# Second attention: low parts of four weight blocks formed on GpSimd in place of VectorE

## The chip, the cores and the metric

One core of one Trainium2 chip runs the whole program: TensorE (PE), VectorE (DVE), ScalarE (ACT), GpSimd (POOL) and SyncE (SP), each with its own instruction stream, kept in step by semaphores. The metric is the device time of one execution in microseconds (us); of several runs the median counts.

## What is computed

A first transformer block (window attention, latent attention, a mixture of 16 experts), then a second block: a state-space mixer, a gated feed-forward network with a short convolution, a forgetting attention ("fox"), another such network, and a final norm. The change lies in the forgetting attention:

```python
def fox_mixer(h, w_in, b_f, w_out):
    proj = h @ w_in
    q = proj[..., :D_MODEL].reshape(Bsz, S, FOX_HEADS, FOX_HEAD_DIM) * (FOX_HEAD_DIM ** -0.5)
    k = proj[..., D_MODEL:2 * D_MODEL].reshape(Bsz, S, FOX_HEADS, FOX_HEAD_DIM)
    v = proj[..., 2 * D_MODEL:3 * D_MODEL].reshape(Bsz, S, FOX_HEADS, FOX_HEAD_DIM)
    f_logit = proj[..., 3 * D_MODEL:]
    log_f = jax.nn.log_sigmoid((f_logit + b_f).astype(f32))
    F = lax.cumsum(log_f, axis=1).transpose(0, 2, 1)
    ...
    def attend_block(args):
        qi, q_blk, Fq = args
        s = jnp.einsum('bhqd,bshd->bhqs', q_blk, k).astype(f32)
        s = s + Fq[..., None] - F[:, :, None, :]
        s = jnp.where(causal, s, -jnp.inf)
        p = jax.nn.softmax(s, axis=-1)
        return jnp.einsum('bhqs,bshd->bqhd', p.astype(v.dtype), v)
    ...
    return o @ w_out
```

with 256 positions, width 1024, 16 heads of 64.

## The kernel before

**Matrices in two parts.** The large float32 products are done as three products of rounded parts: a matrix is its high part (rounded to the format fp32r) plus its low part (what the rounding left), and high x high, low x high and high x low are summed in PSUM. For a weight block ScalarE copies the high part (`apart_high`, line 492) and another engine subtracts it to form the low part in the block's own place (`apart_low`, line 500).

**The weight blocks.** They are numbered n in the list `APART`: 0 to 5 belong to the state-space mixer; 6 to 13 to the forgetting attention. Of these 6 and 7 give the queries, 8 and 9 the keys, 10 and 11 the two halves of the values, 12 and 13 the two halves of the output projection. A block is 128 partitions x 4096 float32 (2 MB); both helpers treat it in two halves of 128x2048. All lie in `ring`, a buffer of six slots; a block takes two of them (raw, later low; and high). SyncE loads a block when TensorE has finished with the products of the block that was there before (`released`), so the loads hang on TensorE and not on who forms a low part. `apart_low` waits for `w_high` (ScalarE's half is written) and raises `w_low0` or `w_low1` (by half), which TensorE waits for ahead of the products of that half.

**TensorE's order** in this stage: queries and keys (`features`, eight signals `fox_mm`, which the Vector and Scalar engines wait for to copy the results out of PSUM), then `values(0, 0, ...)` (block 10, first 128 positions), the eight-column product `gate_rows`, `values(1, 0, ...)` (block 11), and then four waits: `fk_copied`, `fv_copied` 2 (ScalarE has copied both value halves), `nf_ready` 8, `gate_copied`. Then `attention(8, 16, ...)` runs eight steps s = 8 to 15 (four heads each: scores, transposes, products with the values). Beside them stand the value products of the last 128 positions (s = 8 to 11) and the output projection of the first 128 positions (`fox_out`, block 12 at s = 13, block 13 at s = 14 and 15).

**VectorE's order**: low parts of 8 and 9; four copies of the keys (line 2734, each behind `fox_mm` 5 to 8), with the low part of 10 between the second and the third; the low part of 11; then the **bias loop**, lines 2741 and 2743: for each of eight pairs of heads it adds the causal mask to the table `nf` of forget sums (128x256 and 128x512 elements, eight times each, all operands in SBUF: `nf` lies in the work buffer `W`, the mask in `kc`) and signals `nf_ready`. In the attention each step does `inverse`, two `probs_copied`, `maxima` of the step after the next, then `between(s)` with low parts of 12 (s = 8, 9) and 13 (s = 12, 13), then `normalized`.

**ScalarE's order**: high parts of 10 and 11, the value copy `values_copied(0)`, high part of 12, gate copy, `values_copied(1)`, then the exponentials; the high part of 13 stands in halves behind the exponentials of s = 11 and s = 12.

**GpSimd** has its last work before this stage in the state-space mixer (lines 2036 and 2044, ending some 300 us earlier).

The order is written out by hand, and each engine takes its instructions in that order.

Of the kernel before, what the change touches and what calls it, by code (L numbers as in the profile page):

```python
# [239 lines left out]
def build(nc, x, cons, cols, rows, relb, wrt, wff, bf16z, w_in, w_qb, w_kvb, w_o, w_gate, w_up, w_down, ada_w,  # L240
# [5 lines left out]
    with ExitStack() as ctx:  # L246
# [5 lines left out]
        def S(name):  # L252
            if name not in sems:
                sems[name] = ctx.enter_context(nc.semaphore(name))
            return sems[name]
# [192 lines left out]
        def low_at(at):  # L448
# [14 lines left out]


        (_, fqT_, fkT_, fv_, nf_, ft_, PT2_, Rf_) = carve(NC * T, NC * T, NC * T, NT * D, FH * 384, 4 * T, 2 * BANK,
                                                          BANK)
        FOX_END = 3 * NC * T + NT * D + FH * 384 + 4 * T + 3 * BANK
# [27 lines left out]
        def apart_low(eng, n, half):  # L495

            name = APART[n]
            a = slice(half * SLOT // 2, (half + 1) * SLOT // 2)
            eng.wait_ge(S("w_high"), 2 * n + half + 1)
            eng.tensor_tensor(ringr[:, slot_of[name], a], ring[:, slot_of[name], a],  # L500
                              ringr[:, high_slot[name], a].bitcast(F32), ALU.subtract
                              ).then_inc(S(f"w_low{half}"), 1)
# [917 lines left out]
        def _(act):  # L1420
# [454 lines left out]
            def fox_high(u):  # L1875

                _, t, half, _ = half_unit(2 * u)
                a, c = slice(t * P, t * P + P), slice(4 * half, 4 * half + 4)
                act.wait_ge(S("o_copied"), 2 * u + 2)
                act.activation(oh[:, c, a], oTf[:, c, a], ACT.Copy).then_inc(S("row_high"), 1)  # L1880
# [23 lines left out]
        def _(pool):  # L1904
# [135 lines left out]
            def kx(ct):  # L2040

                if ct >= 2:
                    pool.wait_ge(S("cy_mm"), ct - 1)
                tt(Kx[:, ct % 2].rearrange("p n (g c) -> p n g c", g=8),
                   Kc[:, ct].unsqueeze(2).to_broadcast([P, SL, 8, S5C]),
                   K("mask8").unsqueeze(1).unsqueeze(3).to_broadcast([P, SL, 8, S5C]), ALU.mult
                   ).then_inc(S("near_ready"), 1)

            for ct in range(NC):
                decay(ct)  # L2050
                kx(ct)


        @block.vector
        def _(v):
# [671 lines left out]
            for half in range(2):  # L2727
                apart_low(v, 9, half)
            for j in range(4):
                if j == 2:  # L2730
                    for half in range(2):
                        apart_low(v, 10, half)
                v.wait_ge(S("fox_mm"), 5 + j)
                v.tensor_copy(fkT[:, 2 * j:2 * j + 2, :], ps[:, 4 + j, :].rearrange("p (c t) -> p c t", c=2)
                              ).then_inc(S("fk_copied"), 1)
            for half in range(2):
                apart_low(v, 11, half)
            v.wait_ge(S("line_spread"), 32)
            for j in range(FH // 2):
                pair = nf[:, 2 * j:2 * j + 2, :]  # L2740
# [6 lines left out]
            def fox_low(u):  # L2747

                _, t, half, _ = half_unit(2 * u)
                a, c = slice(t * P, t * P + P), slice(4 * half, 4 * half + 4)  # L2750
                v.wait_ge(S("row_high"), 2 + u - 3)
                tt(ol[:, c, a], oTf[:, c, a], oh[:, c, a].bitcast(F32), ALU.subtract).then_inc(S("row_low"), 1)

            def fox_between(s):
                if s < 10:
                    apart_low(v, 12, s - 8)
                if s >= 10 and s % 2 == 0:
                    fox_low((s - 2) // 2)
                if s in (12, 13):
                    apart_low(v, 13, s - 12)  # L2760

            attention(8, 16, fox_between)
            fox_low(7)
            for t in range(NT):
# [107 lines left out]
```

## Time and profile before

| | us |
|---|---|
| median of 3 runs | 1361.81 |
| lowest, highest | 1357.71, 1364.49 |
| the profiled execution | 1355.92 |
| its span | 1354.1 |
| TensorE busy in the span | 1202.8 (89%) |
| VectorE busy | 675.1 (50%) |
| ScalarE busy | 449.4 (33%) |
| GpSimd busy | 164.5 (12%) |

The profiled execution lies 5.9 us under the median of the runs. "Busy" is a sum over all stages and tells only who works most; what a change in one stage is worth is read from the stage's own rows: who waits there, for whom, and how long. The stage of the forgetting attention runs from about 1000 us to 1140 us of the span.

### The profile page before, as it was taken

What the parts mean: (1) busy time and instruction counts of PE and PEld (TensorE: products, weight loads), DVE (VectorE), ACT (ScalarE), POOL (GpSimd) and SP (SyncE); (2) the same over time, 40 slices, a digit from 0 to 9 for tenths busy, and PEclk for the clock granted to TensorE, in tenths of its full rate; (3) what the DMA queues carried; (4) which work ended last, traced back from release to release, by engine and by line L of the source; (5) the groups of instructions that cost most, each with busy time, mean ns of one, the idle gap of its engine ahead of it and who ended that gap; (6) DMA issues with size and microseconds to landing.
All of it is one profiled execution on the core that took longest, in us unless ns stands there. A gap on an engine that the chain in (4) does not pass through costs nothing.

```text
span 1354.1 us, 21898 instructions
## 1 busy us (share of the span) xinstructions
PE 1202.8 (89%) x8746; PEld 866.7 (64%) x8746; DVE 675.1 (50%) x1182; ACT 449.4 (33%) x696; POOL 164.5 (12%) x269
## 2 busy tenths in 40 slices
PE   7999889988777988787998979999969987999996
PEld 4645445444233533334866869999959765999995
DVE  2777451212111212214468547666664765677666
ACT  4563412101010100004445244444344444444442
POOL 0000130572343123030110000000000000000000
PEclk9999889878888788778999989999989988999999
DMA  9866899999999999999694235554245222454451
GB/s 363 337 225 265 322 411 427 426 431 427 428 430 427 428 430 427 428 430 389 239 391 182 93 140 186 186 186 186 108 187 205 107 93 94 156 194 184 186 184 43
DMA packets 38100, 371.78 MB, mean 275 GB/s; under 512 B 4102, under 2 KB 7711, under 8 KB 14367
## 3 DMA queue, kind: packets, MB, share of 16 engines
q1 hardware_dynamic: 33552, 364.66, 66.3%
q10 hardware_dynamic: 4494, 6.38, 1.4%
q8 instruction: 38, 0.62, 0.2%
q14 instruction: 16, 0.12, 0.0%
HBM read 369.94 MB, written 1.08 MB: 274 GB/s over the span
## 4 chain that ended last, share of the span: by engine, by line
PE 64%; DMA 25%; DVE 7%; ACT 2%; issue 2%; SPq 0%; DVEq 0%; ACTq 0%
PE ps L666 61%; DMA ring<-in_w_up 21%; DMA ring<-in_ada_w 1%; DMA ring<-in_w_in 1%; PE ps L889 1%; DMA ring<-in_s_out 1%; DMA ring<-in_fox_out 1%; DMA ring<-in_fox_in 1%; PE ps L675 1%; DVE ring_parts L500 1%; DVE W L2743 0%; ACT XH L1487 0%; PE ps L901 0%; DVE XH L2061 0%; DVE W_parts L2658 0%
## 5 line engine op out<-in xcount | busy, mean ns | idle before, releaser
L666 PE MATMUL ps<-W_parts 128*128 128x256 f32 (+2 forms) x2672 | 387.8, 307 | 8.4 <-DVE W_parts L2094 6.1
L666 PEld LDWEIGHTS ps<-W_parts 128*128 128x128 f32 x2672 | 360.6, 193 | 33.5 <-issue 12.0
L666 PE MATMUL ps<-ring,W 128*32 128x512 f32 (+2 forms) x1512 | 238.8, 688 | 55.3 <-DMA ring<-in_w_up 35.0
L666 PEld LDWEIGHTS ps<-ring,W 128*32 128x32 f32 (+1 forms) x1512 | 66.5, 129 | 200.6 <-issue 132.7
L666 PE MATMUL ps<-W 128*32 128x64 f32 (+7 forms) x1696 | 138.6, 298 | 25.3 <-DVE W L2548 14.5
L666 PEld LDWEIGHTS ps<-W 128*32 128x32 f32 (+5 forms) x1696 | 87.6, 157 | 85.4 <-issue 64.4
L2658 DVE TENSOR_TENSOR W_parts<-ring,W_parts 128x2048 fp32r<-128x2048 f32 x44 | 100.9, 2292 | 29.7 <-ACT W_parts L1797 29.7
L666 PE MATMUL ps<-kc,W 128*128 128x32 f32 (+2 forms) x648 | 99.5, 324 | 1.7 <-DVE W L2331 1.0
L666 PEld LDWEIGHTS ps<-kc,W 128*128 128x128 f32 x648 | 99.1, 245 | 2.8 <-DVE W L2331 1.3
L666 PE MATMUL ps<-XH_parts,ring_parts 128*128 128x256 f32 x512 | 94.1, 287 | 5.1 <-issue 5.1
L2537 DVE COPY W<-ps 128x1024 f32<-128x1024 f32 x16 | 19.6, 1224 | 153.8 <-PE ps L666 153.8
L666 PEld LDWEIGHTS ps<-XH_parts,ring_parts 128*128 128x128 f32 x512 | 81.4, 195 | 6.1 <-issue 6.1
L1797 ACT ACTIVATE W_parts<-ring 128x2048 fp32r<-128x2048 f32 x44 | 83.6, 1901 | 0.0
L666 PE MATMUL ps<-ring_parts,W_parts 128*128 128x512 f32 (+1 forms) x256 | 72.7, 403 | 2.2 <-DVE ring_parts L500 2.2
L666 PE MATMUL ps<-W_parts,ring_parts 128*128 128x256 f32 x256 | 73.4, 287 | 0.0
L500 DVE TENSOR_TENSOR ring_parts<-ring,ring_parts 128x2048 fp32r<-128x2048 f32 x28 | 63.1, 2283 | 10.5 <-ACT ring_parts L492 10.5
L492 ACT ACTIVATE ring_parts<-ring 128x2048 fp32r<-128x2048 f32 x28 | 52.1, 1904 | 27.4 <-DMA ring<-in_fox_in 17.3
L1696 ACT ACTIVATE W<-ps 128x1024 f32<-128x1024 f32 x16 | 16.4, 1025 | 133.2 <-PE ps L666 133.2
L2554 DVE TENSOR_TENSOR X<-X,ps 128x512 f32<-128x512 f32 x64 | 44.0, 687 | 28.7 <-PE ps L666 28.7
L666 PEld LDWEIGHTS ps<-ring_parts,W_parts 128*128 128x128 f32 x256 | 49.1, 194 | 13.4 <-DVE ring_parts L500 2.6
L1821 ACT ACTIVATE XH<-ps 128x256 f32<-128x256 f32 x44 | 16.9, 384 | 117.2 <-PE ps L666 117.2
L666 PE MATMUL ps<-ring,silz 128*32 128x512 f32 x384 | 49.8, 641 | 5.2 <-DMA ring<-in_ada_w 5.2
(381 smaller groups left out, 1278.2 us busy)
## 6 DMA issues: line engine op xcount, KB each, us to landing
ring<-in_w_up SPq DMA_DIRECT2D x32, 2048.0 KB, 26.4
ring<-in_w_down SPq DMA_DIRECT2D x32, 2048.0 KB, 21.2
ring<-in_w_gate SPq DMA_DIRECT2D x30, 2048.0 KB, 21.7
ring<-in_ada_w SPq DMA_DIRECT2D x24, 2048.0 KB, 13.1
ring<-in_up SPq DMA_DIRECT2D x44, 1024.0 KB, 5.6
ring<-in_dn SPq DMA_DIRECT2D x44, 512.0 KB, 3.4
ring<-in_fox_in SPq DMA_DIRECT2D x6, 2048.0 KB, 8.6
ring<-in_w_in SPq DMA_DIRECT2D x2, 2048.0 KB, 13.6
```

The lines of the kernel that those rows point to most:

```text
L492: act.activation(ringr[:, high_slot[name], a], ring[:, slot_of[name], a], ACT.Copy).then_inc(S("w_high"), 1)
L500: eng.tensor_tensor(ringr[:, slot_of[name], a], ring[:, slot_of[name], a], ringr[:, high_slot[name], a].bitcast(F32), ALU.subtract).then_i ...
L666: return pe.matmul(o, l, r, start=a, stop=z_, skip_group_check=True, **kw)
L675: last = pe.transpose(ps[:, c // 2, (c % 2) * T + t * P:(c % 2) * T + t * P + P], XN[:, t, c * P:c * P + P], ident)
L889: last = pe.transpose(ps[:, 4 + g % 2, o:o + P], Pex[:, 2 * (g % 4) + h, kb * P:kb * P + P], ident)
L1696: act.activation(Gs.rearrange("p (b n) -> p b n", b=2), ps[:, 0:2, :], ACT.Copy).then_inc(S("g_copied"), 1)
L1797: act.activation(uh[:, b], ring[:, slot_of[name, b], 0:2048].rearrange("p (a n) -> p a n", a=2), ACT.Copy).then_inc(S("up_high"), 1)
L1821: act.activation(apd[:, b, 2:2 + T], ps[:, b, 0:T], ACT.Copy).then_inc(S("a_copied"), 1)
L2537: v.tensor_copy(Us.rearrange("p (b n) -> p b n", b=2), ps[:, 2:4, :]).then_inc(S("u_copied"), 1)
L2554: tt(xs_part, xs_part, ps[:, k, :], ALU.add).then_inc(S("x_added"), 1)
L2658: tt(ul[:, b, :, :], ring[:, slot_of[f"up{k}", b], 0:2 * D].rearrange("p (a n) -> p a n", a=2), uh[:, b, :, :].bitcast(F32), ALU.subtract) ...
```

## The change

The low parts of blocks 10 to 13 (eight instructions of 128x2048) leave VectorE and stand at the end of GpSimd's stream, in the order of the blocks. GpSimd first waits until both halves of all ten earlier low parts are done, so that the counts `w_low0` and `w_low1` keep rising in order.

```diff
@@ GpSimd, at its end
             for ct in range(NC):
                 decay(ct)
                 kx(ct)
+            for half in range(2):
+                pool.wait_ge(S(f"w_low{half}"), 10)
+            for n in range(10, 14):
+                for half in range(2):
+                    apart_low(pool, n, half)
@@ VectorE
             for j in range(4):
-                if j == 2:
-                    for half in range(2):
-                        apart_low(v, 10, half)
                 v.wait_ge(S("fox_mm"), 5 + j)
                 v.tensor_copy(fkT[:, 2 * j:2 * j + 2, :], ps[:, 4 + j, :].rearrange("p (c t) -> p c t", c=2)
                               ).then_inc(S("fk_copied"), 1)
-            for half in range(2):
-                apart_low(v, 11, half)
             v.wait_ge(S("line_spread"), 32)
...
             def fox_between(s):
-                if s < 10:
-                    apart_low(v, 12, s - 8)
                 if s >= 10 and s % 2 == 0:
                     fox_low((s - 2) // 2)
-                if s in (12, 13):
-                    apart_low(v, 13, s - 12)
```

VectorE ahead of the bias loop, before the change (`L500` is a low part, `L2734` a copy of the keys, `L2741` and `L2743` the bias loop):

```order
L500 TENSOR_TENSOR ring_parts<-ring,ring_parts 128x2048 [waits w_high] x2
L2734 COPY W<-ps 128x512 [waits fox_mm] x2
L500 TENSOR_TENSOR ring_parts<-ring,ring_parts 128x2048 [waits w_high] x2
L2734 COPY W<-ps 128x512 [waits fox_mm] x2
L500 TENSOR_TENSOR ring_parts<-ring,ring_parts 128x2048 [waits w_high] x2
L2741 TENSOR_TENSOR W<-W,kc 128x2x128 [waits line_spread]
L2743 TENSOR_TENSOR W<-W,kc 128x2x256 [waits dve_own]
```

The same place after it (line numbers are shifted by one or a few; `L2740` and `L2742` are the bias loop):

```order
L500 TENSOR_TENSOR ring_parts<-ring,ring_parts 128x2048 [waits w_high] x2
L2735 COPY W<-ps 128x512 [waits fox_mm] x4
L2740 TENSOR_TENSOR W<-W,kc 128x2x128 [waits line_spread]
L2742 TENSOR_TENSOR W<-W,kc 128x2x256 [waits dve_own]
```

The four copies now stand together, and the bias loop follows them directly.

The end of GpSimd's stream after the change (`L2036` and `L2044` are the last work of the state-space mixer, the last rows of before):

```order
L2036 COPY W<-mag 128x4x63 [waits rot_out]
L2044 TENSOR_TENSOR W<-W,kc 128x512 [waits cy_mm]
L500 TENSOR_TENSOR ring_parts<-ring,ring_parts 128x2048 [waits w_high,w_low1,w_low0]
L500 TENSOR_TENSOR ring_parts<-ring,ring_parts 128x2048 [waits w_high] x7
```

Eight subtractions have come to its end, each waiting only for ScalarE's high part of its half. TensorE's, ScalarE's and SyncE's streams are unchanged.

## Rows read from the trace of the kernel before

**Rows 1.** The page, part 1: busy time, share, instructions.

```profile
PE 1202.8 (89%) x8746; PEld 866.7 (64%) x8746; DVE 675.1 (50%) x1182; ACT 449.4 (33%) x696; POOL 164.5 (12%) x269
```

**Rows 2.** Chain that ended last, 1057 to 1071 us: start, us, what.

```profile
1057.46 0.69 DVE W L2734
1058.15 4.40 DVE ring_parts L500 x2
1062.55 0.35 DVE W L2741
...
1071.06 0.25 issue
```

**Rows 3.** Timeline of ScalarE: start, us, instruction, [idle before, releaser].

```profile
1043.90 3.72 ACT L492 ACTIVATE ring_parts<-ring 128x2048 fp32r<-128x2048 f32 x2 [4.86 <-DMA ring<-in_fox_in]
1054.41 3.72 ACT L492 ACTIVATE ring_parts<-ring 128x2048 fp32r<-128x2048 f32 x2 [6.78 <-DMA ring<-in_fox_in]
...
1065.53 3.72 ACT L492 ACTIVATE ring_parts<-ring 128x2048 fp32r<-128x2048 f32 x2 [1.87 <-DMA ring<-in_fox_out]
...
1070.45 0.60 ACT L1865 ACTIVATE W<-ps 128x512 f32<-128x512 f32 x1 [0.29 <-PE ps L666]
...
1093.92 1.92 ACT L492 ACTIVATE ring_parts<-ring 128x2048 fp32r<-128x2048 f32 x1 [4.54 <-DMA ring<-in_fox_out]
```

**Rows 4.** Timeline of TensorE, 1057 to 1072 us.

```profile
1057.26 0.40 PE L666 MATMUL ps<-ring_parts,XH_parts 128*128 128x512 f32 x1
...
1064.56 0.48 PE L666 MATMUL ps<-ring_parts,XH_parts 128*128 128x512 f32 x1
...
1071.31 0.94 PE L666 MATMUL ps<-W 64*128 64x128 f32 x12 [0.89 <-DVE W L2743]
```

**Rows 5.** GpSimd's groups by shape, whole span: count, busy us, mean ns, idle before.

```profile
L1983 POOL TENSOR_SCALAR W<-W,kc 128x512 f32<-128x512 f32 x16 | 24.8, 1563 | 0.8
...
L1939 POOL TENSOR_TENSOR W<-W 128x1024 f32<-128x1024 f32 x1 | 2.4, 2367 | 0.1
...
L1934 POOL TENSOR_TENSOR W<-W 128x1024 f32<-128x1024 f32 x1 | 1.9, 1910 | 0.0
...
L1939 POOL TENSOR_TENSOR W<-W 128x512 f32<-128x512 f32 x1 | 1.3, 1255 | 0.1
```

**Rows 6.** Timeline of GpSimd, state-space mixer.

```profile
684.11 1.57 POOL L2044 TENSOR_TENSOR W<-W,kc 128x512 f32<-128x512 f32 x1 [3.52 <-PE ps L666]
...
704.80 1.07 POOL L2044 TENSOR_TENSOR W<-W,kc 128x512 f32<-128x512 f32 x1 [10.34 <-PE ps L666]
...
727.32 1.40 POOL L2044 TENSOR_TENSOR W<-W,kc 128x512 f32<-128x512 f32 x1 [9.99 <-PE ps L666]
```

**Rows 7.** Timeline of VectorE, state-space mixer.

```profile
679.37 0.42 DVE L2624 TENSOR_TENSOR W<-W 128x256 f32<-128x256 f32 x1
...
683.47 1.29 DVE L2620 TENSOR_TENSOR W<-XH,W 128x512 f32<-128x512 f32 x2
684.79 1.17 DVE L2624 TENSOR_TENSOR W<-W 128x256 f32<-128x256 f32 x1
...
726.57 1.22 DVE L2605 TENSOR_TENSOR W_parts<-XH,XH_parts 128x1024 fp32r<-128x1024 f32 x1
727.71 1.29 DVE L2598 TENSOR_TENSOR XH<-W 128x256 f32<-128x256 f32 x1
```

**Rows 8.** Timeline of VectorE, attention steps.

```profile
1081.50 0.42 DVE L2254 TENSOR_TENSOR W<-ps,W 128x256 f32<-128x256 f32 x1 [1.97 <-PE ps L666]
...
1106.20 0.42 DVE L2254 TENSOR_TENSOR W<-ps,W 128x256 f32<-128x256 f32 x1 [0.82 <-PE ps L666]
...
1117.17 0.42 DVE L2254 TENSOR_TENSOR W<-ps,W 128x256 f32<-128x256 f32 x1 [3.25 <-PE ps L666]
```

**Rows 9.** Windows: stretch, length, PE, PEld, DVE, ACT, POOL busy, PEclk, DMA share, GB/s.

```profile
1076.00:1078.00 2.00, 2.00 (x8) 1.62 (x7) 1.94 (x11) 1.52 (x8) 0.00 (x0) 0.50 0.04 8
...
1104.00:1106.00 2.00, 1.88 (x16) 1.60 (x16) 1.38 (x1) 1.99 (x9) 0.00 (x0) 0.50 0.00 0
```

## The prediction

> **What bounds the kernel now.** I read the page's busy times first: TensorE is busy 1202.8 of 1354.1 us [rows 1], so another engine counts only where TensorE waits for it. Then I read the chain of waits through the forgetting attention. Up to 1057.46 it is TensorE's products; then it passes to VectorE: the last key copy, the two low halves of block 11 (4.40 us), and from 1062.55 the bias loop, which ends at 1071.06 [rows 2]. That looks like an invitation: take 4.4 us of low parts off VectorE just there. So I next read who else would hold TensorE at that point. TensorE's own timeline shows the first value product at 1057.26, the second from 1064.56, and the first scores at 1071.31, with 0.89 us of idle ahead of them [rows 4]. ScalarE begins the copy of the second value product at 1070.45 and needs 0.60, so it ends at 1071.05 [rows 3]. The scores wait for that copy too. The bias loop and the copy end within 0.01 us of each other: the 4.4 us are covered by value products all but completely.
>
> **What the change removes.** Eight instructions of 2.2 us each, 17.6 us of VectorE's work. Those of block 10 lie between key copies that wait for TensorE. Those of block 11 are the 4.40 us above; without them, and with nothing put in their place, the bias loop (8.51 us, from 1062.55 to 1071.06) could run from 1058.15 to 1066.7, and the start of the scores would still be held at 1071.05 by ScalarE's copy. Gain 0.01 us. Those of blocks 12 and 13 stand in attention steps, and behind each VectorE is idle until TensorE's next result: 1.97 us after the first of block 12, 0.82 and 3.25 us after those of block 13 [rows 8]. Gain nothing. So the best that can come of it is no change.
>
> **What it adds: eight long GpSimd instructions.** No GpSimd row has 2048 elements. A subtraction or sum of two whole tensors took 1.255 us for 512 and 2.367 us for 1024 [rows 5]. Each further 512 costs 1.11, which gives 4.6 us for 2048; I take 4.5. The bounds: the cheapest row of 1024 elements took 1.91 [rows 5], twice that is 3.8; the dearest kind, 1.563 for 512 [rows 5], would give 6.2 for 2048. ScalarE's high parts set when each can start: a pair of halves takes 3.72, so the first half is there 1.9 after the pair begins. For blocks 10, 11 and 12 the first halves are there at 1045.8, 1056.3 and 1067.4, the second 1.8 later [rows 3].
>
> Is TensorE late for these? Block 10: 1045.8 to 1054.8, wanted from 1057.26 on [rows 4]: in time by 2.4. Block 11: first half at 1060.8, wanted at 1064.56. Second half at 1065.3 or a little later, wanted in the middle of the second value product, about 1067.5. In time, by some 2 us.
>
> **What it does to VectorE beside them.** This is the term that decides. In the state-space mixer GpSimd's 128x512 product takes 1.07 us where VectorE is idle, at 704.80. At 684.11 it took 1.57 [rows 6]. VectorE was then in the second of two L2620 products, begun at 683.47, both of whose operands lie in SBUF. VectorE's next one, L2624, begun at 684.79, took 1.17 where it took 0.42 at 679.37 [rows 7]. Both figures fit one reading: GpSimd waited until L2620 was done (684.7), then worked to 685.7, and L2624 waited for it. It happens again at 727.32: GpSimd took 1.40 [rows 6], until L2605 was done at 727.7 plus its own 1.05; and L2598, which follows L2605, took 1.29 for 128x256 elements [rows 7]. So the two don't share, they take turns by whole instructions, and a waiting GpSimd comes ahead of VectorE's next instruction. This concerns VectorE instructions with two operands in SBUF; each of the bias loop's sixteen is such a one.
>
> The Trainium skill says the same ("SBUF — State Buffer", section "SBUF: two separate sides"): VectorE and GpSimd have one pair of ports in common, an exclusive lock for a whole instruction, and a VectorE instruction with two SBUF inputs asks for it. It adds no price; the trace agrees with the 1.17 and 1.29 us above.
>
> Now in order of time, with 4.5 for GpSimd:
> - 1056.3: GpSimd begins block 11, first half, to 1060.8. VectorE's bias loop could begin at 1058.15 [rows 2] but waits.
> - 1060.8: one bias instruction (0.4), then GpSimd's second half, 1061.3 to 1065.8.
> - 1065.8: the bias loop runs for four instructions or so, until block 12 is there at 1067.4 and its turn comes at about 1067.8.
> - 1067.8 to 1072.3 GpSimd; one bias instruction; 1072.9 to 1077.4 GpSimd.
> - Ten bias instructions are left: five pairs of 8.51/8 = 1.06, 5.3 us. With 0.1 to start, the loop ends at 1082.8.
>
> The sum doesn't hang on the turns: 1056.3 + 4 x 4.5 + 8.5 = 1082.8, as long as GpSimd always has the next half ready or the loop runs meanwhile. Against 1071.06 that is **11.7 us** later, and nothing covers it: TensorE has no other work ahead of the scores, and all later work, the loads of block 13 and of the next network's weights among it, hangs on TensorE.
>
> **The clock.** TensorE's granted clock is 0.50, its lower level of 1.2 GHz, from 1076 to 1078, after some microseconds of light work, and again from 1104 to 1106 after an idle stretch [rows 9]. With 12 us of idle it will be at the lower level when the scores begin, some 5 us of the chain earlier than now. TensorE works only a part of that time, 12 instructions of 0.94 us in all at the start of it [rows 4], and then mostly waits. Bounds 0 and 2.6 us; I take 0.7, since the rest waits for other engines.
>
> **Block 13** is formed beside the steps s = 12 and 13. Its high half begins at 1093.92 and takes 1.92 [rows 3], so GpSimd would hold the ports from 1095.8 to 1100.3, and again after the second half, both moved by the 12 us. Between these VectorE has short instructions on SBUF alone. The rows that follow show slack of 0.82 and 3.25 us [rows 8], and low parts of 2.2 us each have gone from the same steps. I count 0, at most 1.
>
> **Sum.** 11.7 + 0.7 = 12.4 us. The profiled execution would take 1355.9 + 12.4 = 1368.3; the median of the runs lies 5.9 above it, so the forecast is 1361.8 + 12.4 = **1374.2 us**, 0.9% slower.
>
> **Rivals.**
> - *No turns in this place, so not slower.* GpSimd's subtraction and the bias loop run side by side. Then the scores begin when ScalarE's value copy ends: 0 to 0.01 us gained, 1361.8. It decides as long as block 11's second half is there by 1067.5, as worked out above. For it: only 128x512 GpSimd instructions are seen to block. Against: four inflated durations above, all of instructions of the same kind as here. 0.12.
> - *VectorE keeps its turn.* If the bias loop, once begun at 1060.8, lets nobody in, it ends at 1069.4. Block 11's second half then runs from 1069.4 to 1073.9, and TensorE's second half of that product (2.9 us) ends at 1076.8, ScalarE's copy at 1077.4, scores at 1077.7: 6.4 later, 1368.2. Against it: GpSimd came ahead of VectorE's next instruction at both places. 0.08.
> - *A dearer GpSimd instruction.* At 6.2 us block 10 ends at 1058.2, block 11 at 1071, four beyond TensorE's need, and block 12 at 1084; the bias loop ends near 1090: 19 later, 1381. 0.12.
> - *Faster after all*: the attention steps gain from a lighter VectorE more than the rows show, or the clock comes out kinder. 0.04.
> - The forecast: 0.64.
>
> The Trainium skill bears on the price as well ("GPSIMD Engine Reference", section "Elementwise — side-by-side cycle accounting"): it gives 4.497 us for a float32 sum of 2048 elements. By it the sum would be the same 12.4, and the dearer instruction would be out. No row here shows that size.
>
> **How the numbers follow.** About 0.5% (6.8 us) is what a measurement of this kernel can tell from no change. Slower by more: the forecast and the dearer instruction, 0.76, less a little for noise: 0.75. Within: no turns and VectorE first, 0.20. Faster: 0.05. The range runs from 1365, just under the case of +6.4, to 1381, the dearer instruction; left out are no turns and faster, 0.16.
>
> **What would show it.** In the profile after, TensorE idle ahead of the first scores: some 12 to 13 us, put down to VectorE's bias loop; some of the sixteen bias instructions with a duration near 5 us, four of them; GpSimd's eight at about 4.5 us, or more where they wait for VectorE; granted clock 0.50 at the first scores. I am wrong if the bias instructions keep 0.42 and 0.69 us, or if TensorE's idle stands inside the second value product in place of behind it.

## The result, and the profile after

| | before | changed |
|---|---|---|
| median of 12 runs, us | 1359.02 | 1371.00 |
| lowest to highest | 1351.47 to 1364.49 | 1367.24 to 1376.67 |
| the profiled execution | 1355.92 | 1372.41 |
| its span | 1354.1 | 1370.6 |

The changed kernel is slower: the ratio is 1.0088, with a 95% interval of 1.0069 to 1.0107, or 12.0 us between the medians. The forecast was 12.4 us more, 1374.2 us in all. Most of the 3.2 us between that and 1371.00 is the base: the forecast was counted from a median of three runs, 1361.81, and the twelve runs have 1359.02.

The two profiled executions differ by 16.5 us. Part of that has nothing to do with the change: TensorE's first value product starts at 1057.26 us before [rows 4] and at 1061.32 after, and ahead of it both kernels do the same but for block 10, for which no one waited. 3.36 of these 4.06 us are there already when TensorE begins the norm of this stage (1000.42 and 1003.78), and the profiled executions of the experiments below start the first value product anywhere from 1057.11 to 1068.87. So from here on all is measured from TensorE's first value product, in two lengths: up to the first scores, and up to the start of the next network's norm on VectorE (1140.48 before, 1156.05 after).

| | first value product to first scores | to the next norm |
|---|---|---|
| before | 14.05 | 83.22 |
| changed | 25.50 | 94.73 |
| difference | 11.45 | 11.51 |

At the end of the stretch the price is what it was at the first scores, so I look there. (In between it is up to 1.7 us more; that is the clock's part, told further down.) The timeline of TensorE in the changed kernel, where [rows 4] has an idle time of 0.89:

```profile
1061.32 0.40 PE L666 MATMUL ps<-ring_parts,XH_parts 128*128 128x512 f32 x1
...
1068.63 0.48 PE L666 MATMUL ps<-ring_parts,XH_parts 128*128 128x512 f32 x1
...
1086.82 2.08 PE L666 MATMUL ps<-W 64*128 64x128 f32 x16 [12.34 <-DVE W L2742]
```

TensorE idles 12.34 us, and what it waits for is the bias loop (lines 2740 and 2742 now). The second value product begins 7.31 us after the first, as before (7.30): TensorE never waited for block 11 itself. The timeline of GpSimd:

```profile
1050.35 9.14 POOL L500 TENSOR_TENSOR ring_parts<-ring,ring_parts 128x2048 fp32r<-128x2048 f32 x2 [317.29 <-ACT ring_parts L492]
1060.67 9.34 POOL L500 TENSOR_TENSOR ring_parts<-ring,ring_parts 128x2048 fp32r<-128x2048 f32 x2 [1.19 <-ACT ring_parts L492]
1071.23 9.48 POOL L500 TENSOR_TENSOR ring_parts<-ring,ring_parts 128x2048 fp32r<-128x2048 f32 x2 [1.22 <-ACT ring_parts L492]
1112.62 4.55 POOL L500 TENSOR_TENSOR ring_parts<-ring,ring_parts 128x2048 fp32r<-128x2048 f32 x1 [31.91 <-ACT ring_parts L492]
1118.56 4.52 POOL L500 TENSOR_TENSOR ring_parts<-ring,ring_parts 128x2048 fp32r<-128x2048 f32 x1 [1.39 <-ACT ring_parts L492]
```

and of VectorE at the same time:

```profile
1061.52 0.69 DVE L2735 COPY W<-ps 128x512 f32<-128x512 f32 x1 [2.14 <-PE ps L666]
1062.13 3.45 DVE L2740 TENSOR_TENSOR W<-W,kc 128x256 f32<-128x256 f32 x1
1065.61 4.95 DVE L2742 TENSOR_TENSOR W<-W,kc 128x512 f32<-128x512 f32 x1
1070.49 0.41 DVE L2740 TENSOR_TENSOR W<-W,kc 128x256 f32<-128x256 f32 x1
1070.93 0.69 DVE L2742 TENSOR_TENSOR W<-W,kc 128x512 f32<-128x512 f32 x1
1071.54 4.81 DVE L2740 TENSOR_TENSOR W<-W,kc 128x256 f32<-128x256 f32 x1
1076.39 4.87 DVE L2742 TENSOR_TENSOR W<-W,kc 128x512 f32<-128x512 f32 x1
1081.18 0.41 DVE L2740 TENSOR_TENSOR W<-W,kc 128x256 f32<-128x256 f32 x1
```

Four of the sixteen bias instructions last 3.45 to 4.95 us, the other twelve keep 0.41 and 0.69. In each long one the time over its own is GpSimd's. They take turns: GpSimd holds 1060.67 to about 1065.2, one bias instruction gets through (it ends at 1065.58), GpSimd's second half, one bias instruction (to 1070.56), two more while GpSimd waits for ScalarE's high part of block 12, then the same pattern again. The key copy at 1061.52, which reads PSUM, keeps its 0.69 although GpSimd is at work.

### The profile page after: what moved, and what is told of

It is laid out like the page before. It is cut to its first block, busy times and chain, and to the rows that moved or that the text cites. A ratio compares the mean times of both kernels' runs of the same rounds, so it can differ in the third digit from the quotient of the medians.

```text
span 1370.6 us, 21899 instructions
## 1 busy us (share of the span) xinstructions
PE 1205.9 (88%) x8746; PEld 866.3 (63%) x8746; DVE 676.7 (49%) x1174; ACT 449.2 (33%) x696; POOL 202.1 (15%) x277
## 4 chain that ended last, share of the span: by engine, by line
PE 62%; DMA 26%; DVE 7%; ACT 2%; issue 2%; SPq 0%; DVEq 0%; ACTq 0%
PE ps L666 60%; DMA ring<-in_w_up 23%; DVE W L2742 1%; DMA ring<-in_w_in 1%; PE ps L675 1%; DMA ring<-in_ada_w 1%; DVE W L2740 1%; PE ps L889 1%; DMA ring<-in_s_out 1%; DMA ring<-in_fox_in 1%; DMA ring<-in_fox_out 1%; ACT XH L1487 1%; ACT ring_parts L492 0%; DVE XH L2065 0%; PE ps L901 0%
## 5 line engine op out<-in xcount | busy, mean ns | idle before, releaser
L666 PE MATMUL ps<-ring,W 128*32 128x512 f32 (+2 forms) x1512 | 241.7, 694 | 59.0 <-DMA ring<-in_w_up 38.7
L666 PE MATMUL ps<-kc,W 128*128 128x32 f32 (+2 forms) x648 | 95.5, 316 | 1.7 <-DVE W L2335 1.0
L666 PEld LDWEIGHTS ps<-kc,W 128*128 128x128 f32 x648 | 94.8, 236 | 2.8 <-DVE W L2335 1.3
L500 POOL TENSOR_TENSOR ring_parts<-ring,ring_parts 128x2048 fp32r<-128x2048 f32 x8 | 37.0, 4645 | 353.0 <-ACT ring_parts L492 353.0
## 6 DMA issues: line engine op xcount, KB each, us to landing
ring<-in_ada_w SPq DMA_DIRECT2D x24, 2048.0 KB, 13.1
```

What stands on the lines that cost most here:

```text
L666: return pe.matmul(o, l, r, start=a, stop=z_, skip_group_check=True, **kw)
```

## The experiments

The theory was: VectorE instructions with two operands in SBUF and GpSimd's instructions take turns, one whole instruction each; a GpSimd instruction that runs while VectorE wants to start one costs VectorE up to its whole length; the change puts four of them (18 us) onto the bias loop, whose end TensorE waits for. Rivals: the added waits and counts cost; GpSimd slows all VectorE's work a little; part of the price lies at the later steps.

All medians and ratios against the kernel before on the same chip:

| run | median | before | ratio (95%) | to first scores | to s = 11 | to next norm |
|---|---|---|---|---|---|---|
| only block 11 | 1361.32 | 1359.40 | 1.0010 (0.9991 to 1.0029) | 17.07 | 40.14 | 86.86 |
| only block 12 | 1366.02 | 1359.40 | 1.0057 (1.0028 to 1.0086) | 22.60 | 46.13 | 91.54 |
| blocks 10 and 13 | 1357.54 | 1359.40 | 0.9981 (0.9953 to 1.0008) | 14.04 | 36.12 | 81.60 |
| all four, mask in PSUM | 1362.89 | 1359.40 | 1.0008 (0.9986 to 1.0029) | 13.89 | 39.58 | 85.17 |
| block 12 after the loop | 1367.11 | 1358.38 | 1.0057 (1.0032 to 1.0081) | 16.77 | 44.09 | 89.59 |
| mask in PSUM, 12 back | 1358.85 | 1358.38 | 1.0005 (0.9983 to 1.0028) | 13.87 | 35.92 | 82.69 |
| scores first | 1354.35 | 1358.38 | 0.9972 (0.9953 to 0.9992) | (order changed) | 31.82 | 77.30 |
| scores first, all on VectorE | 1359.47 | 1358.38 | 1.0003 (0.9981 to 1.0025) | (order changed) | 36.22 | 81.54 |

The ratio is as the measurement gives it, not the quotient of the two medians. Only three rows have an interval clear of 1: only block 12, block 12 after the loop, and scores first. For the others the argument rests on the stretches, each read from one profiled execution.

"To s = 11" ends at TensorE's short product of line 901 in the fourth attention step (36.09 before, 49.22 in the changed kernel). It is there because of what follows it: around step s = 13 every profile has a stretch at TensorE's lower clock level, and that dip lasts 6.8 us before, with only block 11, and with the mask in PSUM and 12 back, but 3.4 us in all the other profiles, the changed kernel's among them. One of these, scores first with all on VectorE, has no low part on GpSimd at all, so the shorter dip isn't the change's doing. It is worth 1.2 us: from the start of step s = 13 to its output projection 6.05 us pass before and 4.82 in the run with blocks 10 and 13. The last column holds that difference, the one ahead of it doesn't.

**One block at a time.** Three runs share the change out. Only block 11 (10, 12 and 13 stay where they were):

```diff
@@ GpSimd, at its end
+            for half in range(2):
+                pool.wait_ge(S(f"w_low{half}"), 11)
+            for half in range(2):
+                apart_low(pool, 11, half)
@@ VectorE
-            for half in range(2):
-                apart_low(v, 11, half)
...
+                if s == 8:
+                    for half in range(2):
+                        v.wait_ge(S(f"w_low{half}"), 12)
                 if s < 10:
                     apart_low(v, 12, s - 8)
```

> Only block 11 is formed on GpSimd; 10, 12 and 13 stay on VectorE as before. Measured by the stretch from TensorE's first value product to its first scores (14.05 us before, 25.50 after the change). Theory (GpSimd and the bias loop take turns by whole instructions): both long instructions run while the loop wants to, the loop ends at 1056.3 + 9.1 + 8.5, so the stretch is 17.0 us (+2.9), two bias instructions last near 5 us, and the time is about 3 us above before. Rival A (the delay comes from the waits and counts the change added, not from the ports): the same small delay whichever block is moved, no long bias instruction. Rival B (GpSimd's share slows VectorE evenly): all sixteen bias instructions are longer, none is near 5 us.

Measured: 17.07 us to the first scores (17.0 expected), 3.02 over before. Two bias instructions are long, the rest are not, as VectorE's timeline shows:

```profile
1065.33 3.58 DVE L2743 TENSOR_TENSOR W<-W,kc 128x256 f32<-128x256 f32 x1
1068.95 4.96 DVE L2745 TENSOR_TENSOR W<-W,kc 128x512 f32<-128x512 f32 x1
1073.83 0.41 DVE L2743 TENSOR_TENSOR W<-W,kc 128x256 f32<-128x256 f32 x1
```

The loop began 4.4 us earlier than before and lost 7.4. Only block 12:

```diff
@@ GpSimd, at its end
+            for half in range(2):
+                pool.wait_ge(S(f"w_low{half}"), 12)
+            for half in range(2):
+                apart_low(pool, 12, half)
@@ VectorE
-                if s < 10:
-                    apart_low(v, 12, s - 8)
...
+                if s == 12:
+                    for half in range(2):
+                        v.wait_ge(S(f"w_low{half}"), 13)
                 if s in (12, 13):
                     apart_low(v, 13, s - 12)
```

> Only block 12 is formed on GpSimd; 10, 11 and 13 stay on VectorE as before. Theory: the bias loop starts where it did and is broken into twice, each time for 4.55 us, so the stretch from the first value product to the first scores is 14.05 + 9.2 = 23.2 us and the time about 9 to 10 us above before, though block 12's low part isn't wanted until some 35 us later. Rival A: no delay, since nobody waits for block 12 there. Rival B: sixteen evenly slowed instructions.

Measured: 22.60, 8.55 over before; 0.6 less than expected. VectorE's timeline shows the loop in the middle of its work when GpSimd comes:

```profile
1067.39 0.69 DVE L2747 TENSOR_TENSOR W<-W,kc 128x512 f32<-128x512 f32 x1
1068.00 4.80 DVE L2745 TENSOR_TENSOR W<-W,kc 128x256 f32<-128x256 f32 x1
1072.84 4.87 DVE L2747 TENSOR_TENSOR W<-W,kc 128x512 f32<-128x512 f32 x1
1077.63 0.41 DVE L2745 TENSOR_TENSOR W<-W,kc 128x256 f32<-128x256 f32 x1
```

The two are longer by 4.38 and 4.18 us. A GpSimd instruction of 4.55 costs VectorE 4.2 to 4.4, not 4.6. And this block's low part isn't needed until the output projection some 35 us on: work for whose result nobody waits here makes this stretch 8.55 us longer, and the kernel's median 6.6 us (ratio 1.0057). The two prices together are 3.02 + 8.55 = 11.57, the changed kernel's 11.45. Blocks 10 and 13 then have to be free:

```diff
@@ GpSimd, at its end
+            for half in range(2):
+                pool.wait_ge(S(f"w_low{half}"), 10)
+            for half in range(2):
+                apart_low(pool, 10, half)
+            for half in range(2):
+                pool.wait_ge(S(f"w_low{half}"), 13)
+            for half in range(2):
+                apart_low(pool, 13, half)
@@ VectorE
-                if j == 2:
-                    for half in range(2):
-                        apart_low(v, 10, half)
...
             for half in range(2):
+                v.wait_ge(S(f"w_low{half}"), 11)
+            for half in range(2):
                 apart_low(v, 11, half)
...
-                if s in (12, 13):
-                    apart_low(v, 13, s - 12)
```

> Blocks 10 and 13 are formed on GpSimd, 11 and 12 on VectorE as before. Theory: block 10 meets only key copies out of PSUM, which ask for no common port, and block 13 meets short instructions with slack behind them; the stretch stays 14.05 us, and the time is that of before within 1 us. Rival A (the added waits cost): as slow as any other variant. Rival C (part of the 12 us of the change comes from block 13 in the attention steps): up to 1 us slower at steps s = 12 and 13.

Measured: 14.04, as before to 0.01, with the same kind of waits added and twice as many GpSimd instructions as in either run above. The waits cost nothing, so the first rival falls; and the second falls with the unchanged bias instructions next to the long ones. The whole stretch came out 1.6 us shorter than before, which I did not expect. Up to s = 11 nothing is gained (36.12 against 36.09); 0.4 us comes at s = 12, where every other profile is also 0.4 to 0.7 us shorter than the one of before, and 1.2 at s = 13, with the shorter dip. This is before, in windows (stretch, length, busy times, then PEclk, DMA share, GB/s):

```profile
1104.00:1110.00 6.00, 5.88 (x33) 4.43 (x34) 3.57 (x6) 1.99 (x9) 0.00 (x0) 0.50 0.00 0
1110.00:1113.00 3.00, 3.00 (x15) 2.49 (x15) 2.91 (x10) 0.39 (x1) 0.00 (x0) 0.99 0.00 0
```

TensorE was at its lower level for 6 us of work there. In the run with the mask in PSUM and block 12 back (below) the dip is as long, though block 13 is on GpSimd there too. What decides between the two lengths wasn't tested.

**The operands.** The sharpest test of the theory leaves all four blocks on GpSimd and changes only where VectorE reads the mask:

```diff
@@ VectorE, on top of the changed kernel
+            mask_ps = ps[:, 4, 0:T]
             for j in range(4):
+                if j == 2:
+                    v.wait_ge(S("fk_copied"), 1)
+                    own(v.tensor_copy(mask_ps, K("mask")))
...
-                own(tt(pair[:, :, T:T + P], pair[:, :, 0:P], K("mask")[:, P:T].unsqueeze(1).to_broadcast([P, 2, P]),
+                own(tt(pair[:, :, T:T + P], pair[:, :, 0:P], mask_ps[:, P:T].unsqueeze(1).to_broadcast([P, 2, P]),
                        ALU.add))
-                tt(pair[:, :, 0:T], pair[:, :, 0:T], K("mask").unsqueeze(1).to_broadcast([P, 2, T]), ALU.add
+                tt(pair[:, :, 0:T], pair[:, :, 0:T], mask_ps.unsqueeze(1).to_broadcast([P, 2, T]), ALU.add
```

> The changed kernel whole, but VectorE first copies the causal mask (128x256) into a free PSUM bank, and the bias loop reads it there: each bias instruction then has one operand in SBUF in place of two, the same work otherwise. Theory: they no longer ask for the common port, keep 0.42 and 0.69 us, the loop ends near 1066.7 in before's time, the scores wait for ScalarE's value copy, the stretch is 14.05 us, and the time is that of before within 1 us, 12 us under the change. Rival (GpSimd's traffic in SBUF slows VectorE whatever its operands): as slow as the change, with long bias instructions.

Measured: 13.89 to the first scores. The bias instructions are as short as they ever were, though all sixteen begin while GpSimd is at work on block 11 (the first at 1069.68, the last at 1077.51). Block 12 comes when the loop is over, at 1078.20. The timeline of GpSimd:

```profile
1068.55 9.18 POOL L500 TENSOR_TENSOR ring_parts<-ring,ring_parts 128x2048 fp32r<-128x2048 f32 x2 [1.24 <-ACT ring_parts L492]
1078.64 9.06 POOL L500 TENSOR_TENSOR ring_parts<-ring,ring_parts 128x2048 fp32r<-128x2048 f32 x2 [0.92 <-ACT ring_parts L492]
```

VectorE's groups by shape:

```profile
L2746 DVE TENSOR_TENSOR W<-W,ps 128x512 f32<-128x512 f32 x8 | 5.5, 688 | 0.3
L2744 DVE TENSOR_TENSOR W<-W,ps 128x256 f32<-128x256 f32 x8 | 3.3, 414 | 0.0
```

in the changed kernel the same two groups were

```profile
L2742 DVE TENSOR_TENSOR W<-W,kc 128x512 f32<-128x512 f32 x8 | 14.0, 1746 | 0.3
L2740 DVE TENSOR_TENSOR W<-W,kc 128x256 f32<-128x256 f32 x8 | 10.8, 1345 | 0.0
```

Same elements, same results, same GpSimd work; the sixteen are shorter by 15.9 us (eight times 1746 - 688 ns and eight times 1345 - 414). Of these, 7.3 are block 11's two collisions, which the operand in PSUM takes away though GpSimd works beside the loop as before; the other 8.6 are block 12's, which the loop, now not held up, escapes by being done in time. The rival, that GpSimd's traffic slows VectorE whatever its operands, falls. But I had expected the time of before within 1 us, and the stretch is 85.17, 2 us over (3.5 us over up to s = 11). VectorE's timeline after the first scores shows one line out of place:

```profile
1084.25 0.29 DVE L2206 CUSTOM_DVE_ANT_0 XH<-ps,W 128x128 f32<-128x128 f32 x1
...
1084.58 3.15 DVE L2220 TENSOR_SCALAR ngm<-mx 128x4 f32<-128x4 f32 x1
...
1088.60 0.17 DVE L2220 TENSOR_SCALAR ngm<-mx 128x4 f32<-128x4 f32 x1
```

The negated maximum, four elements per partition, one tensor operand, lasts 3.15 us in place of 0.17, until GpSimd's second half of block 12 is done (1087.70). So it isn't only instructions with two SBUF operands. The Trainium skill has this too ("SBUF — State Buffer", section "Who interferes with whom"): VectorE also contends for the common ports with an instruction in a two-port mode, which a copy, a cast and a tensor_scalar can enter. The trace agrees: this TENSOR_SCALAR of four elements is held up, and so is a copy of 128x256 from SBUF to SBUF (1.18 us in place of 0.29, at 1114.03).

**Both kinds.** Two runs tell what this second kind is worth. In one, GpSimd leaves the bias loop alone with block 12 and comes right after it:

```diff
@@ GpSimd, on top of the changed kernel
             for n in range(10, 14):
+                if n == 12:
+                    pool.wait_ge(S("nf_ready"), FH // 2)
                 for half in range(2):
                     apart_low(pool, n, half)
```

> The changed kernel, but GpSimd waits for the whole bias loop before it forms block 12. Theory: only block 11's two instructions collide with the loop, so TensorE's first value product to first scores is 17.0 us (14.05 before, 25.50 in the changed kernel). Block 12's two then run beside the first attention steps, where VectorE's short instructions with SBUF on both sides (the negated maximum, 3.15 us in place of 0.17 in the run with the mask in PSUM; the spread of the denominators) wait for them: the whole stretch from the first value product to the next network's norm (83.2 before, 94.7 changed) becomes 88 to 91. Rival (only instructions with two SBUF operands are held up): 86.8, as with block 11 alone.

Measured: 16.77 and 89.59. The loop now meets only block 11, and yet the stretch is 6.4 us over before, in the expected range of 88 to 91, and 8.0 over at s = 11. The lines of VectorE's timeline:

```profile
1081.00 2.51 DVE L2222 TENSOR_SCALAR ngm<-mx 128x4 f32<-128x4 f32 x1
...
1084.38 3.60 DVE L2222 TENSOR_SCALAR ngm<-mx 128x4 f32<-128x4 f32 x1
```

Two instructions of 0.17 us become 6.1 us together, each with the exponentials and TensorE behind it. Against the run with block 11 alone the stretch is 2.7 longer; up to s = 11 it is 3.95, and the shorter dip hides the rest. In the other run block 12 goes back to VectorE, with the mask in PSUM:

```diff
@@ GpSimd, against the run with the mask in PSUM
-            for n in range(10, 14):
-                for half in range(2):
-                    apart_low(pool, n, half)
+            for half in range(2):
+                apart_low(pool, 10, half)
+            for half in range(2):
+                pool.wait_ge(S(f"w_low{half}"), 11)
+            for half in range(2):
+                apart_low(pool, 11, half)
+            for half in range(2):
+                pool.wait_ge(S(f"w_low{half}"), 13)
+            for half in range(2):
+                apart_low(pool, 13, half)
@@ VectorE
+                if s == 8:
+                    for half in range(2):
+                        v.wait_ge(S(f"w_low{half}"), 12)
+                if s < 10:
+                    apart_low(v, 12, s - 8)
```

> Mask in PSUM, blocks 10, 11 and 13 on GpSimd, block 12 back on VectorE. The run with the mask in PSUM and all four blocks on GpSimd kept a remainder of 2 us over before in this stage, behind one negated maximum of 3.15 us that waited for block 12's second half. Theory: with block 12 gone from there, nothing is left of the change's price: first value product to first scores 13.9 us, the whole stretch 83.2 us or up to 1.6 less, time that of before. Rival (the remainder has another cause, such as the clock or the mask in PSUM): 85 us.

Measured: 13.87 and 82.69, ratio 1.0005 (0.9983 to 1.0028). Nothing is left of the price, with six of the eight instructions still on GpSimd. And nothing is gained either, as the prediction said of the best case: the bias loop is over at 1066.43, and the scores wait for ScalarE's value copy (line 1865), which ends at 1070.89, 0.09 us ahead of them. The timelines of ScalarE and TensorE:

```profile
1070.29 0.60 ACT L1865 ACTIVATE W<-ps 128x512 f32<-128x512 f32 x1 [0.73 <-PE ps L666]
1070.98 1.16 PE L666 MATMUL ps<-W 64*128 64x128 f32 x16 [0.73 <-issue]
```

TensorE's row names nobody for its 0.73 us of idle; that it waits for the copy I read from the two times.

**Can the freed 4.4 us be used?** Only if TensorE has something to do with an earlier end of the bias loop. For that I changed the order on TensorE and ScalarE:

```diff
@@ TensorE
-                scores(first)
-                scores(first + 1)
...
+                    if s == first:
+                        pe.wait_ge(S("fv_copied"), 2)
...
-            values(0, 0, 0, 0, NC)
+            pe.wait_ge(S("fk_copied"), 3)
+            values(0, 0, 6, 0, NC)
+            pe.wait_ge(S("fk_copied"), 4)
+            scores(8)
             gate_rows(2, (2, 3))
-            values(1, 0, 1, 0, NC)
-            pe.wait_ge(S("fk_copied"), 4)
-            pe.wait_ge(S("fv_copied"), 2)
+            values(1, 0, 7, 0, NC // 2)
+            pe.wait_ge(S("gate_copied"), 3)
+            scores(9)
+            values(1, 0, 7, NC // 2, NC)
             pe.wait_ge(S("nf_ready"), FH // 2)
-            pe.wait_ge(S("gate_copied"), 3)
@@ ScalarE
-                act.activation(fv[:, t, BANK * n:BANK * n + BANK], ps[:, 7 if t else n, :], ACT.Copy
+                act.activation(fv[:, t, BANK * n:BANK * n + BANK], ps[:, 7 if t else 6 + n, :], ACT.Copy
...
             values_copied(0)
-            apart_high(act, 12)
...
+            exponentials(8)
+            exponentials(9)
             values_copied(1)
...
             for s in range(8, 16):
-                exponentials(s)
+                if s > 9:
+                    exponentials(s)
+                if s in (10, 11):
+                    apart_high(act, 12, (s - 10,))
@@ VectorE
-                if s < 10:
-                    apart_low(v, 12, s - 8)
+                if s == 10:
+                    for half in range(2):
+                        v.wait_ge(S(f"w_low{half}"), 12)
+                if s in (10, 11):
+                    apart_low(v, 12, s - 10)
```

with block 11 on GpSimd and the mask in PSUM; the wait for `fv_copied` 2 stands behind the scores of s = 10.

> A version meant to be faster. Mask in PSUM; only block 11 on GpSimd; block 12's parts are formed at steps 10 and 11 (high part on ScalarE behind the exponentials, low part on VectorE); value products go to PSUM banks 6 and 7, which the key copies have left, so that TensorE does the scores of steps 8 and 9 before and in the middle of the second value product, and ScalarE does their exponentials before it copies that product. Expected: the bias loop ends near 9.4 us after the first value product, maxima and exponentials of the first two steps run beside the second value product, TensorE has no idle stretch there and keeps its upper clock level: first value product to the next norm 79 us in place of 83.2, about 4 us under before. Rival (another wait takes its place, ScalarE's or the block 13 load's): 82 or more.

Measured: 77.30 us to the next norm, 5.9 under before, and a median of 1354.35 against 1358.38, ratio 0.9972 (0.9953 to 0.9992). It beats both kernels. Of the 5.9 us, 4.3 are there at s = 11 (31.82 against 36.09), about what I expected (4); the rest comes at s = 12 and with the shorter dip. TensorE's windows over the place where before had its idle time and its lower clock:

```profile
1065.00:1075.00 10.00, 10.00 (x63) 7.94 (x62) 6.83 (x29) 6.27 (x20) 3.44 (x1) 1.00 0.19 81
1075.00:1080.00 5.00, 5.00 (x37) 3.72 (x35) 1.99 (x12) 3.72 (x11) 0.00 (x0) 1.00 0.00 0
```

Busy without a gap, at the upper level of 2.4 GHz throughout. Is that the order alone?

```diff
@@ GpSimd, against the run with scores first
-            for half in range(2):
-                pool.wait_ge(S(f"w_low{half}"), 11)
-            for half in range(2):
-                apart_low(pool, 11, half)
@@ VectorE
+            for half in range(2):
+                apart_low(v, 11, half)
...
-                tt(pair[:, :, 0:T], pair[:, :, 0:T], mask_ps.unsqueeze(1).to_broadcast([P, 2, T]), ALU.add
+                tt(pair[:, :, 0:T], pair[:, :, 0:T], K("mask").unsqueeze(1).to_broadcast([P, 2, T]), ALU.add
```

> The same reordering as the version with scores first, but all low parts on VectorE and the mask in SBUF as before: it tells the gain of the order from the gain of moving block 11. Expected: the bias loop ends where it does before, 13.8 us after the first value product, the first exponentials come about 1 us earlier than before since ScalarE no longer copies ahead of them; the stretch to the next norm is 81.5 to 82.5 us, 1 to 2 under before, and 2 to 3 above the version with block 11 on GpSimd. Rival (moving block 11 brings nothing even then): both versions alike.

Measured: 81.54, and no difference in the median (1.0003). The 81.54 lies in the expected range, but not for the expected reason. Up to s = 11 the new order alone gains nothing: line 901's product there starts 36.09 us after the first value product before, 31.82 with scores first, and 36.22 with scores first and all on VectorE. The three rows, in that order:

```profile
1093.35 0.44 PE L901 MATMUL ps<-kc,W 128*128 128x128 f32 x2
1091.89 0.44 PE L901 MATMUL ps<-kc,W 128*128 128x128 f32 x2
1099.57 0.44 PE L901 MATMUL ps<-kc,W 128*128 128x128 f32 x2
```

The first exponentials do come 1.1 us earlier (14.98 us after the first value product, 16.07 before), but the first such product then waits 0.94 us for the value copy that now stands behind them. The 1.7 us at the norm come at s = 12 and with the shorter dip, which this kernel shares with others. Moving block 11, the mask in PSUM with it, is worth 4.4 us up to s = 11 in this order (4.2 at the norm), all that its low part takes from VectorE. In the old order the same move, with blocks 10 and 13 moved too, was worth 0.2 (35.92 against 36.09). The same move with two results is the clearest sign that a cover decided (other work that holds TensorE just as long), and not the move.

## Why the prediction was right

**The bound.** "The 4.4 us are covered by value products all but completely": shown. With the collision taken away (mask in PSUM, 12 back) the first scores start 13.87 us after the first value product, 0.18 earlier than before; 0.01 was forecast. The rest is in the step from the last result to TensorE's start: 0.25 us behind VectorE's loop [rows 2], 0.09 behind ScalarE's copy.

**GpSimd's instruction.** Taken 4.5, measured 4.55 and 4.52 for block 13's two, 4.645 on the mean of all eight, waits for turns included. The line through 512 and 1024 elements [rows 5] gave 4.6; the bound of 6.2, from another kind of operation, was far off. Followed turn by turn, that rival's bias loop ends at 1091.5, not 1090, so its time would have been 1382 and not 1381; nothing hangs on it.

**Turns.** The two rows of inflated durations [rows 6, 7] carried the argument, and it held to the order of turns: GpSimd, one bias instruction, GpSimd. The loop had two free instructions between blocks 11 and 12 and not four, which doesn't alter the sum. Worked out 1082.8, that is 25.5 us after the first value product; measured 1086.57 - 1061.32 = 25.25.

**The rivals.** No turns: falls with the four long instructions. VectorE keeps its turn: falls with the same rows, no more than one bias instruction got in between two of GpSimd's that were ready. Dearer instruction: falls. The price on VectorE per GpSimd instruction for which it waited from start to end is 4.2 to 4.4, slightly under its length; the 0.6 us by which the run with only block 12 came out under its expectation are that.

**The clock.** I took 0.7 within 0 to 2.6. The windows of the changed kernel:

```profile
1074.50:1086.80 12.30, 0.00 (x0) 0.01 (x1) 11.86 (x12) 1.88 (x2) 6.21 (x2) 0.58 0.00 0
1086.80:1096.00 9.20, 7.72 (x37) 5.90 (x38) 4.40 (x31) 5.22 (x25) 0.00 (x0) 0.50 0.01 3
```

After the idle stretch TensorE works at the lower level for some 10 us; the sixteen score products alone take 2.08 us, where before they took 1.16 (the 0.94 of [rows 4] stops at its window's end, after twelve of them). The next products beside the attention start 12.68 us late, 1.2 more than the scores, and those of the next step 13.1. So the term measured 1.2 to 1.7, inside its bounds but about twice the 0.7 taken. At s = 12 the delay is 12.6, and at the output projection of s = 13 it is 11.5 again, because the second dip was shorter in this run. That the two cancel is luck, and so is how near 12.4 lies to the measured 12.0 and 11.51: up to s = 11 the change costs 13.1 us in this profile.

**Block 13.** Counted at 0. Right in the sum, and the reason given (slack behind) holds: VectorE's timeline in the changed kernel has

```profile
1119.93 3.17 DVE L2220 TENSOR_SCALAR ngm<-mx 128x4 f32<-128x4 f32 x1
```

3 us over its own time, and the run with blocks 10 and 13 shows no price for the same. What I had missed is the second kind of instruction that asks for the ports; I had counted only those with two SBUF operands, named the others "short instructions on SBUF alone", and given them up to 1 us. At the first attention steps, without slack, the same kind cost 3.5 us up to s = 11 (mask in PSUM, over before) and 4.0 (block 12 after the loop, over only block 11). In the changed kernel block 12 is done at 1080.71 and the bias loop at 1086.57, so it never met them.

## What to carry to other kernels

Before moving elementwise work to an idle GpSimd, list what VectorE does in the same microseconds: here a TENSOR_TENSOR with two SBUF operands, and a TENSOR_SCALAR or a copy from SBUF to SBUF, stopped until the GpSimd instruction was done, however small they were and whether or not anyone waited for GpSimd's result. Long GpSimd instructions belong beside VectorE work that reads an operand from PSUM, and a constant operand can be copied to a free PSUM bank to make it so. And taking an instruction off the chain of waits pays only as far as the next engine in line is done before it; here the chain named VectorE, and ScalarE's copy ended 0.01 us ahead of it. All of this was seen with one kind of GpSimd instruction, a subtraction that reads and writes SBUF.

## What the runs showed of the hardware

- A GpSimd subtraction of 128x2048 float32 takes 4.50 to 4.64 us where it need not wait for a turn (4.55 and 4.52 for block 13 in the changed kernel), VectorE's 2.29.
- With both engines busy they alternate, one instruction each. A waiting VectorE instruction shows a long duration, not idle time, so a busy share hides it: VectorE's busy time in the whole span rose from 675.1 to 676.7 us though eight low parts had left it (their group went from 63.1 to 45.0 us).
- A VectorE TENSOR_SCALAR of 128x4 elements from SBUF to SBUF is held up like a large one (3.60 us in place of 0.17); the spread copy of 128x256 also (1.19 in place of 0.29). Copies out of PSUM (0.69), sums with one operand in PSUM (0.41 and 0.69), the maxima with one operand in PSUM (0.29) and, though it goes from SBUF to SBUF, the reciprocal of 128x4 (0.17) kept their times beside GpSimd.
